# Two more samples' value pages summed by ScalarE and VectorE, with whole-page products, in a one-core decoder layer

## What is computed

```
k_past = cache_k[l][page_table].reshape(DB, past_len, A_HEADS, A_DH)
v_past = cache_v[l][page_table].reshape(DB, past_len, A_HEADS, A_DH)
...
p = jax.nn.softmax(logits, axis=-1)
...
o = (jnp.einsum('bhqsj,bhqsjd->bqhd', p_sel, vs)
     + jnp.einsum('bhqj,bhjd->bqhd', p_own, v_own))
```

## Time and profile before

| | |
|---|---|
| median of 3 runs | 2679.09 us (2676.86 to 2682.29) |
| the profiled execution, its own time | 2678.82 us |
| its span, first to last instruction | 2676.8 us |
| TensorE busy | 2647.9 us, 99% of the span |
| VectorE busy | 1588.5 us, 59% |
| ScalarE busy | 1129.0 us, 42% |
| chain that ended last | 94% TensorE, 2% DMA, 2% VectorE |

### The profile page before, as it was taken

How to read it: one execution, slowest core, us unless ns; L and a number is a source line. 1 busy time by engine, 2 the same in 40 slices (tenths; PEclk the granted TensorE clock), 3 DMA queues, 4 the chain that set the end, 5 groups by cost and what they waited for, 6 DMA issues and landing times.

```text
span 2676.8 us, 50707 instructions
## 1 busy us (share of the span) xinstructions
PE 2647.9 (99%) x21524; PEld 2586.9 (97%) x21524; DVE 1588.5 (59%) x2582; ACT 1129.0 (42%) x1113; POOL 147.6 (6%) x266
## 2 busy tenths in 40 slices
PE   8999999999999999999999999999999999999998
PEld 7899999999999999999999988999999999999998
DVE  4554555445557768786685776565545554555555
ACT  6433333333335433455353476544433333333345
POOL 0000000000000011112111122000000000000000
PEclk9999999999999999999999999999999999999999
DMA  7665555555555799799989799676555555565543
GB/s 264 235 215 182 179 185 178 187 175 188 176 173 169 235 303 299 249 340 392 336 290 334 272 335 365 217 230 188 174 179 182 180 183 184 176 185 177 188 153 116
DMA packets 487450, 600.07 MB, mean 224 GB/s; under 512 B 12608, under 2 KB 447008, under 8 KB 485984
## 3 DMA queue, kind: packets, MB, share of 16 engines
q1 hardware_dynamic: 442512, 456.37, 52.9%
q0 software_dynamic: 35088, 129.74, 13.2%
q10 hardware_dynamic: 9680, 11.54, 1.2%
HBM read 575.16 MB, written 24.53 MB: 224 GB/s over the span
## 4 chain that ended last, share of the span: by engine, by line
PE 94%; DMA 2%; DVE 2%; ACT 1%; issue 1%; DVEq 0%; POOLq 0%; ACTq 0%
PE PS L555 29%; PE PS L556 29%; PE PS L557 29%; DVE splitL L510 1%; PE PS L591 1%; PE PS L592 1%; PE PS L593 1%; DMA raw<-w_gate 1%; DMA ring<-cache_v 1%; ACT splitH L504 1%; PE PS L2065 0%; PE PS L1780 0%; DMA mtok<-mem_prompt 0%; PE PS L1498 0%; PE PS L1748 0%
## 5 line engine op out<-in xcount | busy, mean ns | idle before, releaser
L510 DVE TENSOR_TENSOR splitL<-raw,splitH 128x2048 fp32r<-128x2048 f32 (+1 forms) x462 | 1007.3, 2180 | 801.4 <-ACT splitH L504 800.4
L504 ACT ACTIVATE splitH<-raw 128x2048 fp32r<-128x2048 f32 (+1 forms) x462 | 844.1, 1828 | 1464.2 <-PE PS L557 1417.6
L555 PE MATMUL PS<-gH,splitH 128*128 128x264 f32 x3072 | 880.8, 287 | 4.6 <-DVE splitL L510 4.6
L556 PE MATMUL PS<-gL,splitH 128*128 128x264 f32 x3072 | 871.5, 284 | 0.0
L557 PE MATMUL PS<-gH,splitL 128*128 128x264 f32 x3072 | 870.8, 283 | 0.0
L555 PEld LDWEIGHTS PS<-gH,splitH 128*128 128x128 f32 x3072 | 579.7, 189 | 18.5 <-issue 18.2
L556 PEld LDWEIGHTS PS<-gL,splitH 128*128 128x128 f32 x3072 | 580.1, 189 | 0.6 <-issue 0.2
L557 PEld LDWEIGHTS PS<-gH,splitL 128*128 128x128 f32 x3072 | 577.0, 188 | 0.0
L555 PE MATMUL PS<-hH,splitH 128*128 128x264 f32 x1536 | 436.1, 284 | 0.1
L556 PE MATMUL PS<-hL,splitH 128*128 128x264 f32 x1536 | 435.1, 283 | 0.0
L557 PE MATMUL PS<-hH,splitL 128*128 128x264 f32 x1536 | 434.9, 283 | 0.0
(11 more groups left out here) (384 smaller groups left out, 3039.9 us busy)
## 6 DMA issues: line engine op xcount, KB each, us to landing
raw<-ffn_w SPq DMA_DIRECT2D x240, 1024.0 KB, 5.1
raw<-w_in SPq DMA_DIRECT2D x64, 1024.0 KB, 6.8
raw<-w_gate SPq DMA_DIRECT2D x48, 1024.0 KB, 8.1
ring<-cache_k POOLq DMA_DIRECT2D x64, 512.0 KB, 5.9
ring<-cache_v POOLq DMA_DIRECT2D x64, 512.0 KB, 6.2
raw<-ffn_w SPq DMA_DIRECT2D x32, 768.0 KB, 4.5
raw<-w_out SPq DMA_DIRECT2D x16, 1024.0 KB, 5.4
raw<-w_mem_kv SPq DMA_DIRECT2D x15, 1024.0 KB, 5.5
```

What stands on the lines that cost most here:

```text
L504: nc.scalar.activation(splitH[:, s, tiles, :], raw[:, u, 0:nk, :], ACT.Copy).then_inc(hi_ready, 1)
L510: nc.vector.tensor_tensor(splitL[:, s, tiles, :], raw[:, u, 0:nk, :], splitH[:, s, tiles, :].bitcast(F32), ALU.subtract).then_inc(split_re ...
L555: nc.tensor.matmul(out, w_hi, H[:, k, 0:n], start=first, stop=False)
L556: nc.tensor.matmul(out, w_hi, L[:, k, 0:n], start=False, stop=False)
```

## The change

Samples 1, 2, 3, 4, 5 and 7 take the way over ScalarE and VectorE, samples 0 and 6 stay on TensorE. The pages of the six come two in a unit, an even and an odd one, in four units running, then a unit without. The odd page is no longer done head by head: one product of the page with the probabilities, repeated along each head's 128 columns, in place, then a wait of VectorE on its own semaphore (`link`), then one addition to `vAcc`.

```diff
-    PE_SAMPLES, VEC_SAMPLES = (0, 2, 4, 6), (1, 3, 5, 7)
-    PE_PAIR_AT = (109, 110, 112, 114, 115, 117, 119, 122, 123, 125, 126, 129, 130, 132, 134, 136)
-    VEC_PAGE_AT = (108, 108, 109, 110, 111, 112, 112, 113, 116, 117, 118, 118, 119, 120, 120, 121, 124, 124, 125, 126, 127, 127, 128, 128, 131, 131, 132, 133, 133, 134, 135, 135)
+    PE_SAMPLES, VEC_SAMPLES = (0, 6), (1, 2, 3, 4, 5, 7)
+    PE_PAIR_AT = (109, 112, 115, 118, 124, 127, 130, 133)
+    VEC_PAGE_AT = (108, 108, 109, 109, 110, 110, 111, 111, 113, 113, 114, 114, 115, 115, 116, 116, 118, 118, 119, 119, 120, 120, 121, 121, 123, 123, 124, 124, 125, 125, 126, 126, 128, 128, 129, 129, 130, 130, 131, 131, 133, 133, 134, 134, 135, 135, 136, 136)
...
-        for h in range(A_HEADS):
-            acc = vAcc[:, h * P:(h + 1) * P]
-            last = nc.vector.scalar_tensor_tensor(acc, ring[:, s, h * P:(h + 1) * P], DA["L"][:, k, g, h:h + 1], acc,
-                                                  ALU.mult, ALU.add)
-        last.then_inc(page_used[s], 1)
+        page = ring[:, s, :].rearrange("p (h c) -> p h c", h=A_HEADS)
+        link(nc.vector.tensor_tensor(page, page, DA["L"][:, k, g, :].unsqueeze(2).to_broadcast([P, A_HEADS, P]), ALU.mult))
+        nc.vector.tensor_tensor(vAcc[:, :], vAcc[:, :], ring[:, s, :], ALU.add).then_inc(page_used[s], 1)
```

More of the change, by code:

```diff
@@ L2030, in act_vec_page, with dve_vec_page @@
             last.then_inc(v_prod, 1)
-    def dve_vec_page(dve, k, g):
+    def dve_vec_page(dve, link, k, g):
         page_read(dve, ("V", k, g - 1))
@@ L2431, in dve_side @@
             if g:
-                dve_vec_page(dve, k, g)
+                dve_vec_page(dve, link, k, g)
         if T in ROW_TURN_AT:
```

## The result

| | before | changed |
|---|---|---|
| median of 9 runs | 2678.68 us (2676.86 to 2682.29) | 2686.28 us (2682.85 to 2688.26) |
| ratio of changed to before, 95% interval | | 1.0027 (1.0018 to 1.0035) |
| span of the profiled execution | 2676.8 us | 2684.4 us |
| mean granted clock | 0.997 | 0.994 |

The change makes the kernel 7.6 us slower by the medians. The forecast was 2683.5 us.

What follows compares the result with a forecast made beforehand. The prediction took TensorE as the bound, busy 2647.9 of 2676.8 us. New waits of 14.6 us against 10.2 us saved made it 4.4 us longer, 2683.5 us against the median; range 2674 to 2696 us.

Steps and rivals of the forecast that it cites:

- 112, its split: Unit 112: TensorE waits 0.5 us for a weight split that VectorE does after adding a page and multiplying another.
- 112, the pair: Unit 112: TensorE waits 2.0 us for the pair's second page, whose slot sample 1's page 4 holds.
- 115: Unit 115: TensorE waits 3.8 us for the pair's second page, in the slot of sample 2's page 0, scaled in unit 113.
- 123: Unit 123: TensorE's value sum waits 2.8 us for VectorE's copy of sample 2's row, behind the split for unit 124.
- 127: Unit 127: TensorE waits 5.5 us for the pair's second page, in the slot of sample 4's page 4, scaled in unit 125.
- The relief: TensorE's queue: eight pairs go, 7.8 us; two value sums come, 0.9 us; old page waits of 3.3 us go; 10.2 us saved.
- the clock: Rival: TensorE's clock falls to half in the new waits of units 115 and 127; 16.2 us slower, 2695.3 us; chance 0.16.
- VectorE's room: Units 108 to 126: VectorE's work rises from 80.8 to 104.1 us, as full as TensorE, leaving no cover for late products.
- the three chains of pages: Slot release to page landing for second pages of units 112, 115 and 127: waits of 2.0, 3.8 and 5.5 us.
- Early landing: Rival: pages land in 3.4 us, shortening page waits in units 112, 115 and 127; 3.0 us faster, 2676.1 us; chance 0.22.
- term of 6.75 us: Time from a slot's release to the next page's landing, 0.65 + 6.1 us; called the least sure term.
- The costly product: Rival: VectorE's product with the repeated operand takes 2.19 us instead of 1.22, adding 15.5 us; 2699 us; chance 0.07.

Runs made afterwards that it cites:

- e5: Kernel before with TensorE's four matmuls per page of samples 2 and 4 cut to one of 8 columns: 2676.01 us, ratio 0.9990.
- e3: Changed kernel with TensorE work of no effect filling the time ahead of the waits of units 112, 115, 123 and 127: 2682.20 us, ratio to before 1.0017.
- e10: Changed kernel, same two TensorE samples and whole-page instructions, with other tables for the pairs and for ScalarE's and VectorE's pages: 2672.34 us, ratio to before 0.9975.
- e6: Changed kernel without VectorE's whole-page products of samples 1, 2 and 3 (12 of 24 products): 2681.60 us, ratio to before 1.0008.
- e9: Changed kernel with ScalarE's page product of unit 125 ahead of that unit's evacuation, head turn and exponentials: 2682.13 us, ratio to before 1.0017.
- e12: Changed kernel with half of each value page loaded, 512 of 1024 columns: 2679.83 us, ratio to before 1.0005.
- e8: Kernel before with three instead of four samples on TensorE, whole-page product and addition, and spread tables of its own: 2669.59 us, ratio 0.9963.
- e11: Kernel before with other tables for pairs and pages, nothing moved between engines, its 8 instructions per page kept: 2672.01 us, ratio 0.9982.
- e1: Kernel before with whole-page product and addition in place of the 8 instructions per odd page, samples and tables unchanged: 2679.59 us, ratio 1.0003.
- e2: Changed kernel's samples and tables with the 8 instructions per odd page of before: 2686.54 us, ratio to before 1.0031.

## Why the prediction was right, and where not

- **Sign, range, place.** Slower was forecast by 4.4 us and measured as 7.6, inside the range; the five waits are where the working put them. By unit, forecast and measured (us): 112, its split 0.5 and 0.77; 112, the pair 2.0 and 2.08; 115, 3.8 and 1.49 + 1.52 = 3.0; 123, 2.8 and 0.34 (the turn of a row in unit 122) + 0.63 + 3.42 = 4.4; 127, 5.5 and 1.27 + 3.30 = 4.6. Sum 14.6 and 14.8. None is behind unit 128, as forecast. That the sum is so close is luck: single terms are off by up to 1.6. Of the forecast's own signs one of those for being right failed (VectorE busy for over 100 us in units 108 to 126: 98.3) and one of those for being wrong came (a granted clock under 1.00: 0.97).
- **The relief.** 7.8 less, 0.9 more: the rests of the table bear it out as TensorE's own time (212.9 forecast, 211 to 214 in eight kernels). But e5 shows what it is worth alone, with the tables of before: 2 us.
- **The step that failed: the clock.** It was priced as a rival, at 0.16, and left out of the sum. The term measured 4.4 us by the stage of e3, and 5.5 as what the ledger of the profiled execution lacks (10.1 + 7.8 - 0.9 + 3.3 - 14.8); with it the sum is 9 to 10 us, and the stage grew by 10.1. By the medians what the sum lacked is less, 7.6 - 4.4 = 3.2, and e3 took 3.5 away. The rival's own condition, waits well above the 1.3 us that had left the clock alone, was met by the forecast's own chains of 3.8 and 5.5 us, so the text had no ground to give it so little; its price, 5.9 us for a fall, was three times too high or more: three falls cost 3.2 to 5.5 us together. In e3 the clock did not fall in the stage once the waits were filled (PEclk 1.00 in both stretches). The Trainium skill, TensorE: Matmul & The Clock Gate, Part 1, says that activity lifts the throttled clock, and this agrees with e3.
- **VectorE's room.** The forecast had 104.1 us of work for VectorE in units 108 to 126 and called it as full as TensorE (whose own 104.6 us took five pairs off where the tables take six and bring a sum). It had 98.3 us there, since its last two units of pages run behind TensorE, past 1643 us; and fullness was the wrong word for the limit. VectorE stood 11.2 us for ScalarE's products. With other tables it carried 101.4 us in less time while TensorE waited 5.2 (e10). For the split and row-copy waits it was VectorE's queue (e6); for the page waits it was the release of a slot behind TensorE's own end of unit, which the three chains of pages had named, and e9 shows this for unit 127. For units 112 and 115 it was argued and not tried by itself; in 115 the slot of the second page is that of a sample's first page, which ScalarE may not scale before a sum that TensorE makes in the same unit. The first pages of units 115 and 127 are another matter. Their issues and TensorE's matmuls, 1563.45 to 1572.66 and 1639.88 to 1647.87, are 9.2 and 8.0 us apart: long loads. A first page that had come sooner would have left TensorE to stand as much longer for the second.
- **The rivals.** Early landing: the median was 5.9 us, near the 6.1 that the sum took. But the sum needed the loads of three pages, the second ones of units 112, 115 and 127. Their releases and issues (for unit 127 they are shown above):

```profile
1547.79 1.23 DVE L2038 TENSOR_TENSOR vAcc<-vAcc,ring 128x1024 f32<-128x1024 f32 x1 [1.13 <-ACT ring L2025]
1550.21 0.53 POOL L1671 DMA_DIRECT2D ring<-cache_v  x1 [4.01 <-issue]
1566.30 2.44 ACT L2025 ACTIVATE vAcc<-ring,A_L 128x128 f32<-128x128 f32 x8
1569.96 0.53 POOL L1671 DMA_DIRECT2D ring<-cache_v  x1 [4.91 <-issue]
```

  From issue to TensorE's matmul they took 5.9, 4.8 and 4.4 us, so for two of the three the page did come early. The issue came 1.2 us behind the release in all three, where the sum had 0.65. Its term of 6.75 us measured 7.1, 6.1 and 5.6. The shortest landing in the stage of the change was 3.8 us: the estimate of 3.2 us by the fit in the Trainium skill, DMA: Bandwidth & Descriptors, Anatomy of one DMA — SWDGE (gpsimd) path, is not met. At a median of 4.1 us, with half the bytes (e12), the time was 2679.8, that of before, so the rival's condition, some 4.5 us, was well put; its price of 2676.1 at 3.4 us was not tried. The costly product: 1.225 us, no ground for it.
- **What was not said.** That a sample moved could pay with other tables (e10, e8), and that tables alone would (e11), the forecast did not ask.

## What to carry to other kernels

Work taken off the bounding engine is a gain only if what that engine meets next is ready sooner too: follow each freed slot back through the queues, and look above all for a release that stands behind the bounding engine's own last instruction. Move the order of the pages and the work together; a table that suits one split of the work is not neutral for another. Spreading the pages took 14 us off the change and some 5 to 7 us off the kernel before, where moving the two samples as well added nothing (e10 against e11). Count the clock as a possible price of every wait of TensorE, and read it from PEclk and the count of matmuls in short windows, since busy time doesn't show it.

## What the runs showed of the hardware

How long TensorE stands does not by itself decide whether the clock falls. In e6, one execution, a wait of 2.22 us was followed by a fall and one of 2.39 us was not; in e1 one of 1.79 us was and one of 2.21 was not. The windows around the two of e6:

```profile
1558.00:1560.00 2.00, 2.00 (x11) 2.00 (x11) 1.97 (x5) 0.00 (x0) 1.06 (x2) 0.50 0.96 325
1576.00:1578.00 2.00, 2.00 (x22) 1.68 (x14) 1.97 (x2) 1.53 (x4) 0.00 (x0) 1.00 0.99 340
```

So a wait of 2 us has a price that differs from place to place, 0 or some 1.7 us; one of 2.72 us in e2 was followed by 3.4 us of it. The falls differ from run to run of one kernel as well, as far as the mean granted clock of the whole span tells: in e6 it lay between 0.993 and 0.997 over 12 runs. Halving the pages' bytes took the DMA engines' share in the first window from 0.90 to 0.73 and the median landing only from 5.9 to 4.1 us.
